# Attention of a decoder step: seventeen copies of turned probabilities given to the vector engine, query tiles and small steps in another order

## The reference

```python
def block(i):                       # one tile of 128 queries
    idx = indexer_select(qi, wi, ki, qpos, k_sel)   # top 256 of the causal keys
    valid = idx <= qpos[None, :, None]
    return sparse_attend(q, gather(k, idx), gather(v, idx), valid)

def indexer_select(qi, wi, kidx, qpos, k_sel):
    dots = einsum('bqhd,bsd->bqhs', qi, kidx) * IDX_DIM ** -0.5     # 8 index heads
    score = einsum('bqhs,bqh->bqs', relu(dots), wi)
    score = where(kpos <= qpos, score, -inf)
    return top_k(score, k_sel)[1]

def sparse_attend(q, k_sel, v_sel, valid):          # 8 heads, 4 kv heads, width 64
    s = where(valid, einsum('bqkgd,bqnkd->bqkgn', q, k_sel) * HEAD_DIM ** -0.5, -inf)
    return einsum('bqkgn,bqnkd->bqkgd', softmax(s), v_sel)
```

## Time and profile before

| | |
|---|---|
| time, median of 3 runs | 2797.74 us (2795.54 to 2804.0) |
| profiled execution, its own time | 2784.8 us |
| its span | 2782.8 us |
| instructions | 46845 |
| attention stage in the trace | from about 963 to 1627 us |

### The profile page before, as it was taken

The page is one execution under the profiler, slowest core; times in us unless marked ns, Lnnn a source line. Parts: engine busy times, 40 slices in busy tenths (PEclk is TensorE's granted clock), DMA queues, the critical chain, the costliest instruction groups (busy, mean ns, idle before and its releaser), DMA issues. The chain is left out here.

```text
span 2782.8 us, 46845 instructions
## 1 busy us (share of the span) xinstructions
PE 2623.4 (94%) x16259; PEld 1745.7 (63%) x16260; DVE 1987.9 (71%) x3025; ACT 1546.7 (56%) x2600; POOL 849.7 (31%) x1049
## 2 busy tenths in 40 slices
PE   8999999999999999999999978999989599999988
PEld 6766888988999845555466654555645355444433
DVE  4977943667995398788877637564444699999958
ACT  2134888843777567788888747311100156666636
POOL 3422433223333201234443231013130233333326
PEclk9999999999999999999999999999999599999999
DMA  3312433221444422200210368455451598888767
GB/s 122 113 46 69 147 106 116 64 73 54 140 140 120 159 80 80 65 20 28 84 39 21 92 190 259 167 178 185 141 193 42 223 348 318 349 305 314 278 220 286
DMA packets 241726, 415.59 MB, mean 149 GB/s; under 512 B 31284, under 2 KB 156988, under 8 KB 232586
## 3 DMA queue, kind: packets, MB, share of 16 engines
...
## 5 line engine op out<-in xcount | busy, mean ns | idle before, releaser
L557 PE MATMUL p_ps_acc<-p_x_hi,p_w_hi 128*128 128x352 f32 (+2 forms) x1480 | 526.9, 356 | 2.5 <-DVE p_x_lo L861 2.5
L557 PE MATMUL p_ps_acc<-p_x_lo,p_w_hi 128*128 128x352 f32 (+2 forms) x1480 | 518.0, 350 | 0.0
L557 PE MATMUL p_ps_acc<-p_x_hi,p_w_lo 128*128 128x352 f32 (+2 forms) x1480 | 517.8, 350 | 0.0
L902 DVE SCALAR_TENSOR_TENSOR g_shared<-g_late,p_taps,g_shared 128x1024 f32<-128x1024 f32 x360 | 435.2, 1236 | 8.5
L557 PEld LDWEIGHTS p_ps_acc<-p_x_hi,p_w_hi 128*128 128x128 f32 (+1 forms) x1480 | 275.9, 186 | 51.0 <-issue 22.0
L3502 PE MATMUL e_ps_G<-g_late,e_xT 128*32 128x512 f32 x1312 | 303.0, 600 | 0.5
L3502 PE MATMUL e_ps_G<-l_wgu,e_xT 128*32 x656 | 298.1, 601 | 1.6 <-ACT e_xT L3566 1.5
L3502 PE MATMUL e_ps_G<-g_shared,e_xT 128*32 128x512 f32 x656 | 299.4, 601 | 0.1
L557 PEld LDWEIGHTS p_ps_acc<-p_x_lo,p_w_hi 128*128 128x128 f32 (+1 forms) x1480 | 276.1, 187 | 26.6 <-issue 0.5
L557 PEld LDWEIGHTS p_ps_acc<-p_x_hi,p_w_lo 128*128 128x128 f32 (+1 forms) x1480 | 275.6, 186 | 27.0
L480 POOL CAST p_w_hi<-g_late 128x1024 fp32r<-128x1024 f32 x74 | 98.0, 1324 | 597.4 <-PE p_ps_acc L557 578.7
...
## 6 DMA issues: line engine op xcount, KB each, us to landing
...
```

The source lines that it names most:

```text
L557: m = nc.tensor.matmul(bank(n, tb)[0:rows, 0:width], wp[:, slot, k, 0:rows], xp[:, k, at], start=(k == 0 and i == 0), stop=(k == KD - 1 an ...
L902: ch.mark(nc.vector.scalar_tensor_tensor(dst, src, wt, dst, ALU.mult, ALU.add))
```

## The change

Four things change, all inside the attention stage:

1. **Copies.** `MOVED_BY_VECTOR` names 17 pairs (slot, head). Their turned banks are copied into `pT` by DVE (`move_turned`) and not by ACT; a new semaphore `t_moved` counts these copies, and `bank_free` and `values` wait for it at those places. On DVE the copies stand behind `masked(g + 1, 0)` and ahead of the slot's first table step. They are 34 copies of 124 blocks in all.
2. **Order of tiles.** 0 1 6 7 5 4 14 15 2 3 12 13 10 11 8 9 becomes 0 1 4 5 6 7 15 14 2 3 13 12 10 11 8 9.
3. **Places.** `DOTS_AT` goes from 0 4 23 27 31 35 to 0 4 18 23 31 35; `COUNT_AT`, `CHOOSE_AT`, `EARLY_CHOICE_AT` and `BRANCH_SLOTS` have new entries throughout; 40 of the 64 rows of `TENSOR_ORDER` differ.
4. A gather of weights for the next stage waits for the later of the tiles 10, 11 and the early ones, which is the same slot as before.

No arithmetic is added or taken away: the same matmuls, masks, counts and exps run, at other places, and the copies of 17 heads on another engine.

```diff
-TILES = [0, 1, 6, 7, 5, 4, 14, 15, 2, 3, 12, 13, 10, 11, 8, 9]
+TILES = [0, 1, 4, 5, 6, 7, 15, 14, 2, 3, 13, 12, 10, 11, 8, 9]
-DOTS_AT = [0, 4, 23, 27, 31, 35]
+DOTS_AT = [0, 4, 18, 23, 31, 35]
 EARLY_CHOICE_AT = {
...
-    14: "5.1 5.4 6.2 7.5 8.3 8.4",
+    14: "0.2 1.1 1.4 2.0 2.1 3.0",
...
-BRANCH_SLOTS = [0, 1, 2, 3, 4, 5, 6, 7, 8, 10, 11, 12, 14, 15, 18, 19, 23, 27, 31, 32, 33, 34, 35, 36, 37, 38, 39, 40, 41, 43, 44, 45]
+BRANCH_SLOTS = [0, 1, 2, 3, 4, 5, 6, 7, 8, 9, 10, 11, 12, 13, 14, 15, 16, 20, 22, 23, 26, 29, 30, 32, 33, 34, 35, 36, 38, 39, 42, 49]
...
+MOVED_BY_VECTOR = {(38, 1), (52, 1), (63, 0), (23, 1), (34, 1), (37, 0), (32, 1), (35, 1), (38, 0), (41, 1), (31, 1), (23, 0), (45, 1), (35, 0), (36, 0), (37, 1), (53, 1)}
...
                 def bank_free(n):
                     if n - 3 in at.raw:
                         pe.wait_ge(o_done, at.raw[n - 3] + 1)
+                    elif n - 3 in at.moved:
+                        pe.wait_ge(t_moved, at.moved[n - 3])
...
-                    pe.wait_ge(t_kept, at.kept[at.last_turn(g, 1)])
+                    for x in range(2):
+                        if (g, x) in MOVED_BY_VECTOR:
+                            pe.wait_ge(t_moved, at.moved[at.last_turn(g, x)])
+                        else:
+                            pe.wait_ge(t_kept, at.kept[at.last_turn(g, x)])
...
                 def keep_turned(g, x):
+                    if (g, x) in MOVED_BY_VECTOR:
+                        return
...
+                def move_turned(g, x):
+                    if g:
+                        dve.wait_ge(pv_done, 2 * g)
+                    for a, b in cuts(blocks(g // 4), 4):
+                        n = at.turns[g, x, a // 4]
+                        dve.wait_ge(t_full, n + 1)
+                        nc.vector.tensor_copy(pT[:, x, a:b, :], ps_t[n % 3][:, 0:(b - a) * P].rearrange("p (b q) -> p b q", q=P)).then_inc(t_moved, 1)
...
                     if g + 1 < NSLOT:
                         masked(g + 1, 0)
+                    for x in range(2):
+                        if (g, x) in MOVED_BY_VECTOR:
+                            move_turned(g, x)
                     behind(g, 0)
```

127 lines of the change are left out of this document (65 added, 62 removed), and 12 rows, old and new, of the table COUNT_AT.

## The result

The changed kernel took 2805.35 us, the median of 20 runs (2801.8 to 2814.01), beside 2798.53 us of the kernel before (20 runs, 2792.16 to 2809.66): ratio 1.0025, 95% interval 1.0017 to 1.0033. The forecast was 2794.1. The time lies in its range, but on the other side of the old one. Under the 0.3% that the text named it counts as no change; its interval, though, lies on the slower side.

The account below looks back on a forecast made before the run. PE was taken as the bound, so only its waits could move. Terms 3.5 - 4.5 + 0 + 1.9 - 3 - 1 - 0.5 gave -3.6 us, from a median of 2797.74 to 2794.1; range 2782 to 2808.

Parts of the forecast that it names:

- The load, +1.9: Branch weight loads: piece 16, no longer preceded by slots without a piece, makes PE wait; 1.9 us more.
- The start, +3.5: Slots 0 to 7: 5.7 us more work on a nearly full DVE, partly absorbed, delays PE by 3.5 us.
- Dots and branches in the narrow slots, 0: Slots 8 to 22 take the moved dots and pieces at little idling; 0 us, bounds -2 and +4.
- Dots out of the wide slots, -4.5: Slots 27 to 30 lose their dots, so PE idles less in slots 24 to 31; 4.5 us saved.
- ACT relieved, -3: Slots 32 to 47: slot 38's load wait goes (-1.5) and ACT has less to copy (-1.5).
- the copies, -1: 17 heads' copies on DVE, each 0.13 us slower, but banks need not wait behind ACT's counts; -1 us, bounds -2 and +6.
- 2.4 us if its cover were gone: Slot 23's copies delay the next exp by 2.4 us unless that slot's turn, dots and branch piece cover it.
- The end, -0.5: Slots 55 to 63 keep their order; one copy of slot 63 goes to an idle DVE, saving 0.5 us.
- The clock left as it is: The attention stage's clock, 0.97 or more of full in every stretch, was left unchanged in the sum.
- the branch's loads bind: Rival: pieces in all slots 0 to 16 wait for loads, +4.5 us on the forecast; shares the 0.50 for no change.
- VectorE becomes the bound: Rival: DVE, over 95% busy in slots 0 to 23, makes PE wait; +12 us, median 2810, chance 0.17.

Follow-up runs that it names:

- e5: The changed kernel as it is, run again on chip 0; ratio 0.9995 to the kernel before, stage 657.1 us.
- e9: The changed kernel with the branch pieces of slots 2, 8 and 16 last in their rows, chip 0; ratio 0.9986, stage 653.4 us.
- e14: The changed kernel with GpSimd's gathers of slots 57 to 60 held until later exps, chip 3; ratio 1.0022, stage 658.7 us.
- e15: The changed kernel with the pieces of slots 2, 8 and 16 last and the gathers held, chip 3; ratio 1.0002, stage 648.4 us.
- e1: The changed kernel with only slot 2's branch piece last, as in the kernel before, chip 0; ratio 0.998, stage 657.3 us.
- e11: The changed kernel with VectorE's copies in slot 23 only, the other 15 places on ScalarE, chip 14; ratio 1.0045, stage 665.6 us.
- e2: The changed kernel with no copies on VectorE (empty MOVED_BY_VECTOR), chip 0; ratio 1.0043, stage 666.6 us.
- e7: The kernel before with the changed kernel's VectorE copies at the same 17 places, chip 0; ratio 1.0031, stage 665.6 us.
- e4: The kernel before with slot 2's branch piece ahead of the dots, as in the changed kernel, chip 0; ratio 1.0016, stage 658.9 us.
- e16: The changed kernel as it is, run again on chip 3; ratio 1.0022, stage 663.4 us.
- e18: The changed kernel with the pieces of slots 2, 8 and 16 last, second run, chip 4; ratio 1.0008, stage 657.1 us.

## Why the prediction was wrong

*The load, +1.9, is the step that failed.* The item priced only the pieces that need `y_blk`, and passed over two pieces that follow each other across a slot's boundary, slots 1 and 2. The rows said what that costs, 3.34 us from issue to use. PE waited 2.57 us there, and 7.6 us on weights in all; the sum's items left 6.1 (5.7 + 1.9 - 1.5). What it costs in full is shown by putting the pieces of slots 2, 8 and 16 last: the idle time of the stage falls from 38.4 to 35.1 us on chip 0 (e5, e9) and from 39.5 to 35.5 on chip 3 (e14, e15), below the 38.5 and 38.9 of the kernel before. As it stands, and without the stop of slot 59, the changed kernel idles about as long as the kernel before. So these pieces eat a gain of the size that the sum forecast.

*The start, +3.5.* PE's idle time there grew by 4.6 us. VectorE's 5.7 us of work, of which 3.4 was to reach PE, made PE wait 1.4 us more for row maxima, and 3.3 more where slot 2's piece stands last (5.1 for 1.8 us, e1 and e15): the size was right, and the wait for weights covered part of it. The length grew by 8.5 us; the other 3.9 are PE's busy time at a clock of 0.94 for 0.97, and 2.8 of them are absent where e11 and e14 ran the same instructions.

*Dots and branches in the narrow slots, 0.* With the load's 1.9 it was to be 1.9; idle time in slots 8 to 23 grew by 3.7 us (6.5 and 3.1 for 3.4 and 2.5). Slot 16's wait came, at 0.9 us. Slot 8's is 3.0 us for 2.6, and putting its piece last gave 2.7 us of slots 8 to 15 back (e9 against e5), 1.2 of it idle time.

*Dots out of the wide slots, -4.5.* The idle time fell from 9.6 to 7.1: -2.5. The direction held; four slots with both kinds of work are not four quiet ones.

*ACT relieved, -3, and the copies, -1.* Slots 32 to 47 idle 6.1 us for 9.3, -3.2, and turns waited less for ACT's copies (8.4 for 10.9, and 3.5 of the 8.4 are the stop of slot 59), as forecast. But the size of the copies was wrong both ways. They are worth 9.5 us in the new order (e2 against e5) and cost 9.6 in the old (e7 against e4, slots 8 to 63), of which 6.8 and 7.1 are idle time, with VectorE's copy at 0.68 us for the 0.69 I had put. I added a price per copy; slot 23 shows that what counts there is which instruction stands behind it in the queue. The same slot that I costed at 2.4 us if its cover were gone gave 2.5 us less of waiting in the new order, and cost 2.0 in the old. For the places behind slot 31 the cause isn't traced.

*The end, -0.5.* It was +3.8, 74.0 for 70.2, and on chip 0 it is 68.4. The stop in slot 59 is in no row of the kernel before, so it could not be read from them. Holding the gathers takes it away, 5.5 us (e14 against e16), of which some 3 are idle time (10.1 and 7.0 us in the last stretch of the first trace and of e5).

*The clock left as it is.* The sum put it at nothing. In the first trace 3.1 of the stage's 6.6 us are busy time at a lower clock. Executions of the same rows differ by as much: 618.3, 612.9 and 617.1 us in e9, e15 and e18, whose stages differ only in the last gathers. So how much of it the change brings isn't shown.

Of the rivals, "the branch's loads bind" was the nearest, most of all in slot 2 and slot 8. "VectorE becomes the bound" had its place right (slots 0 to 7) but not its price: DVE was busy for 89% of them, not over 95, and PE and its weight loads waited 1.7 us in all for DVE's copies. Adding the measured terms, the idle time is +4.6 +3.7 -2.5 -3.2 -0.1 +1.0 = +3.5, and with the clock's 3.1 +6.6. On chip 0 the same kernel's stage is 657.1, and it shows no change. A stage of the kernel before there can be estimated from e7's slots 0 to 7 and e4's slots 8 to 63, 656.0 us, idle for 37.3: by this the change costs 1.1 us on that chip.

So the waits for the branch's weights took the forecast gain. What made the kernel slower by 0.25% in the first comparison isn't settled. Without the stop (e14) the stage is 4.7 us shorter than e16's, while the ratio stayed at 1.0022. The code behind the stage is the same in all kernels, and its length in single executions on chip 0 runs from 1121.7 (e7) to 1132.0 us (e4), more than all that the stage has to explain. That the time fell inside the stated range is luck in part: the sum of the terms missed by 7.1 us of idle time and 3.1 of busy time, and the range was wide enough for that.
